# Packing the high and low rows of a 32-token tile into one stationary operand, and laying four weight pieces of the last chunk ahead

## The reference

```
D_MODEL = 2048; SEQ = 1024; DEC_SEQ = 32

y_prompt = y_prompt + rms_norm(jnp.einsum('btm,md->btd', mp, w_out[l]), norm_post[l])
y_sample = y_sample + rms_norm(jnp.einsum('btm,md->btd', ms, w_out[l]), norm_post[l])

def rms_norm(x, gain):
    xf = x.astype(jnp.float32)
    y = xf * lax.rsqrt(jnp.mean(xf * xf, axis=-1, keepdims=True) + NORM_EPS)
    return (y * gain.astype(jnp.float32)).astype(x.dtype)
```

## Time and profile before

| | before |
|---|---|
| median of 3 runs | 2122.13 us (2121.92 to 2123.47) |
| the profiled execution's own time | 2120.78 us |
| its span | 2119.0 us |
| PE busy | 2059.1 us, 97% |
| DVE busy | 1078.6 us, 51% |
| ACT busy | 684.1 us, 32% |
| mean granted TensorE clock | 0.992 |

### The profile page before, as it was taken

The page is one execution under the profiler, slowest core; times in us unless marked ns, Lnnn a source line. Parts: engine busy times, 40 slices in busy tenths (PEclk is TensorE's granted clock), DMA queues, the critical chain, the costliest instruction groups (busy, mean ns, idle before and its releaser), DMA issues.

```text
span 2119.0 us, 31442 instructions
## 1 busy us (share of the span) xinstructions
PE 2059.1 (97%) x13280; PEld 1864.0 (88%) x13280; DVE 1078.6 (51%) x2001; ACT 684.1 (32%) x1226; POOL 9.4 (0%) x28
## 2 busy tenths in 40 slices
PE   4999999999999999999999999999999999999996
PEld 4998989898898989999999999999999978887885
DVE  7457676776777676434233332544244562233224
ACT  6223333333434332323222231433133452222221
POOL 1000000000000000000000000000000000000000
PEclk8999999999999999999999999999999999999998
DMA  6256577675757577122221313121322442336323
GB/s 245 75 116 134 122 160 151 138 152 127 148 128 158 121 160 150 51 66 61 51 76 41 91 37 79 42 51 51 67 50 51 142 171 99 104 127 236 123 78 124
DMA packets 601476, 230.75 MB, mean 109 GB/s; under 512 B 395944, under 2 KB 575928, under 8 KB 599576
## 3 DMA queue, kind: packets, MB, share of 16 engines
q1 hardware_dynamic: 600168, 220.76, 41.6%
q0 software_dynamic: 1168, 7.99, 1.0%
HBM read 167.52 MB, written 64.37 MB: 109 GB/s over the span
## 4 chain that ended last, share of the span: by engine, by line
PE 83%; DVE 10%; ACT 3%; DMA 2%; issue 1%; SPq 0%; DVEq 0%; ACTq 0%
PE ps L853 18%; PE ps L854 17%; PE ps L855 17%; PE ps L1048 6%; PE ps L1047 6%; PE ps L1046 6%; DVE arena L1435 3%; PE ps L944 3%; PE ps L1030 3%; PE ps L963 3%; PE ps L911 2%; PE ps L1001 2%; DVE arena L1429 2%; ACT arena L1226 1%; DVE arena L1443 1%
## 5 line engine op out<-in xcount | busy, mean ns | idle before, releaser
L853 PE MATMUL ps<-act_hi,w_hi 128*128 128x352 f32 x2688 | 885.6, 329 | 9.6 <-DVE arena L1370 5.9
L854 PE MATMUL ps<-act_lo,w_hi 128*128 128x352 f32 x2688 | 870.0, 324 | 0.0
L855 PE MATMUL ps<-act_hi,w_lo 128*128 128x352 f32 x2688 | 869.8, 324 | 0.0
L853 PEld LDWEIGHTS ps<-act_hi,w_hi 128*128 128x128 f32 x2688 | 507.4, 189 | 41.1 <-issue 28.5
L855 PEld LDWEIGHTS ps<-act_hi,w_lo 128*128 128x128 f32 x2688 | 507.7, 189 | 0.0
L854 PEld LDWEIGHTS ps<-act_lo,w_hi 128*128 128x128 f32 x2688 | 507.7, 189 | 0.0
L1346 DVE TENSOR_TENSOR w_lo<-w_raw,w_hi 128x512 fp32r<-128x512 f32 x352 | 240.3, 684 | 335.8 <-ACT w_hi L1204 239.7
L1046 PE MATMUL ps<-w_hi,act_hi 128*128 128x512 f32 x576 | 227.2, 394 | 4.9 <-DVE w_lo L1346 2.9
L1048 PE MATMUL ps<-w_hi,act_lo 128*128 128x512 f32 x576 | 229.4, 398 | 0.0
L1047 PE MATMUL ps<-w_lo,act_hi 128*128 128x512 f32 x576 | 228.6, 397 | 0.0
L1132 ACT ACTIVATE w_hi<-w_raw 128x512 fp32r<-128x512 f32 x224 | 139.3, 624 | 214.0 <-DMA w_raw<-in_w_in_dram 213.9
(11 more groups left out here) (120 smaller groups left out, 1618.0 us busy)
## 6 DMA issues: line engine op xcount, KB each, us to landing
w_raw<-in_w_in_dram SPq DMA_DIRECT2D x176, 256.0 KB, 3.0
w_raw<-in_w_out_dram SPq DMA_DIRECT2D x128, 256.0 KB, 2.7
weight_scratch<-arena SPq DMA_DIRECT2D x216, 128.0 KB, 3.8
arena<-weight_scratch SPq DMA_DIRECT2D x54, 512.0 KB, 4.3
w_raw<-in_w_in_dram SPq DMA_DIRECT2D x96, 128.0 KB, 2.4
arena<-in_x_prompt_dram SPq DMA_DIRECT2D x8, 1024.0 KB, 7.0
out_dram<-arena SPq DMA_DIRECT2D x14, 512.0 KB, 2.9
value_scratch<-arena SPq DMA_DIRECT2D x48, 132.0 KB, 3.4
```

What stands on the lines that cost most here:

```text
L853: mm(bank(g, GN), wh, ah, start=(k == 0), stop=False)
L854: mm(bank(g, GN), wh, al, start=False, stop=False)
L855: last = mm(bank(g, GN), wl, ah, start=False, stop=(k == KT - 1))
```

## The change

- **Two matmuls a piece for the sample's tile.** When chunk 3 is done, tile 0's columns of act_hi are free. ACT copies the sample's high part to columns 0-31 of that place and its low part to columns 32-63 (pair, semaphore paired). For tile 8 one stationary operand, pair_rows, then holds both: a matmul against w_hi and one against w_lo give the high rows' product in PSUM partitions 0-31 and the low rows' in 32-63. The low x low product, which the kernel before leaves out, is now added too. Columns 64-127 are whatever tile 0 left, and their rows are not read.
- **A join.** At each of the four chunk ends ACT copies partitions 32-63 of the bank to the tile's rows of y (low_moved), DVE adds the bank's rows 0-31 (joined), ACT squares from y into the bank, and DVE applies the gain to y.
- **The last chunk's end.** LAST_PIECES is 8: PE goes through pieces 0 to 7 with all tiles, then tile by tile over eight pieces. The last four of these are laid ahead during chunk 6: SP loads them into act_lo's columns of tile 3 (as res_lo), ACT makes their high parts in act_hi's columns of tile 3, DVE their low parts in place (late_piece, late_high, late_low). A lone tile takes these four first and the pieces 8 to 11 of the ring after them (the list alone).
- **Small moves.** The gain's load (gain_chunk) is issued after piece 7 instead of piece 9, and the 96 columns of padding behind act_hi and act_lo, with their two memsets, are gone.

```
-LAST_PIECES = 4
+LATE = 4
+LAST_PIECES = LATE + RING
...
-        act_hi_t = place("act_hi", [P, ACT_N + P - DEC], F32R, ACT_N + P - DEC)
-        act_lo_t = place("act_lo", [P, ACT_N + P - DEC], F32R, ACT_N + P - DEC)
-        act_hi = act_hi_t[:, 0:ACT_N].rearrange("p (k t) -> p k t", k=KT)
-        act_lo = act_lo_t[:, 0:ACT_N].rearrange("p (k t) -> p k t", k=KT)
+        act_hi = place("act_hi", [P, KT, TOK], F32R, ACT_N)
+        act_lo = place("act_lo", [P, KT, TOK], F32R, ACT_N)
+        pair_rows = act_hi[:, :, 0:P]
...
+        def late_part(t, i):
+            return t[:, 4 * i:4 * i + 4, 3 * P:4 * P]
+        def piece_view(ap):
+            return ap.rearrange("p (k c) -> p k c", c=P)
...
+            def late_piece(i):
+                sp.wait_ge(y_done, TILES_BEFORE[NCH])
+                g, n = CHUNKS[-1]
+                sp.dma_start(late_part(res_lo, i),
+                             piece_view(w_out_v[:, KORD[KT - LATE + i], PIECE * n:PIECE * n + PIECE])).then_inc(late_in[i], 16)
...
-                for pos in range(RING, KT):
+                for pos in range(RING, KT if c + 1 < len(CHUNKS) else KT - LATE):
                     out_piece(c, pos)
-                    if pos == 9:
+                    if pos == 7:
                         gain_chunk(c)
                     if c == NCH and pos >= 8:
                         residual(pos - 8)
                     if c == NCH + 1 and pos in (7, 9, 11, 13):
                         late_residual(pos // 2 - 3)
+                    if c == NCH + 2 and pos < RING + LATE:
+                        late_piece(pos - RING)
                 if c + 1 < len(CHUNKS):
...
+            alone = list(range(KT - LATE, KT)) + list(range(KT - LAST_PIECES, KT - LATE))
...
-                t0 = TOK * k + P * TOKSETS[g][j]
-                th, tl = act_hi_t[:, t0:t0 + P], act_lo_t[:, t0:t0 + P]
-                mm(bank(s % 8), th, w_hi[:, slot, :], start=(pos == 0), stop=False)
-                mm(bank(s % 8), th, w_lo[:, slot, :], start=False, stop=False)
-                last = mm(bank(s % 8), tl, w_hi[:, slot, :], start=False, stop=(pos == KT - 1))
-                if pos == KT - 1:
+                tt = TOKSETS[g][j]
+                out, wh, wl = bank(s % 8), w_hi[:, slot, :], w_lo[:, slot, :]
+                if c + 1 == len(CHUNKS) and pos >= KT - LATE:
+                    i = pos - KT + LATE
+                    out, wh, wl = piece_view(out), late_part(act_hi, i), late_part(act_lo, i)
+                end = KT - 1 if c + 1 < len(CHUNKS) else alone[-1]
+                if tt == TT:
+                    if c == NCH and pos == 0:
+                        pe.wait_ge(paired, 2)
+                    mm(out, pair_rows[:, k, :], wh, start=(pos == 0), stop=False)
+                    last = mm(out, pair_rows[:, k, :], wl, start=False, stop=(pos == end))
+                else:
+                    th, tl = act_hi[:, k, P * tt:P * tt + P], act_lo[:, k, P * tt:P * tt + P]
+                    mm(out, th, wh, start=(pos == 0), stop=False)
+                    mm(out, th, wl, start=False, stop=False)
+                    last = mm(out, tl, wh, start=False, stop=(pos == end))
+                if pos == end:
                     last.then_inc(y_done, 1)
                 elif j == len(TOKSETS[g]) - 1:
...
-                    for pos in range(KT - by_tile, KT):
-                        if j == 0:
+                    for pos in alone if by_tile else ():
+                        if j == 0 and pos < KT - LATE:
                             pe.wait_ge(lo_made, P3 + KT * c + pos + 1)
+                        elif j == 0:
+                            pe.wait_ge(late_lo, pos - KT + LATE + 1)
                         out_mm(c, pos, j)
...
+                out, src = y[0:rows, j, PIECE * n:PIECE * n + PIECE], bank(s % 8, 512, rows)
                 act.wait_ge(y_done, s + 1)
-                fn(y[0:rows, j, PIECE * n:PIECE * n + PIECE], bank(s % 8, 512, rows), ACT.Square,
+                if tt == TT:
+                    fn(out, ps[DEC:2 * DEC, 512 * (s % 8):512 * (s % 8) + 512], ACT.Copy).then_inc(low_moved, 1)
+                    act.wait_ge(joined, n + 1)
+                    out, src = src, out
+                fn(out, src, ACT.Square,
                    accum_out=ssq_y[0:rows, 4 * tt + n:4 * tt + n + 1]).then_inc(y_sq, 1)
+            def late_high(i):
+                act.wait_ge(late_in[i], 16)
+                fn(late_part(act_hi, i), late_part(res_lo, i), ACT.Copy).then_inc(late_hi, 1)
+            def pair(src, at):
+                act.wait_ge(y_done, TILES_BEFORE[NCH])
+                fn(act_hi[:, :, at:at + DEC], src[:, :, SEQ:TOK].bitcast(F32), ACT.Copy).then_inc(paired, 1)
             def following_high(c, pos):
-                if pos + RING < KT:
+                if pos + RING < (KT if c + 1 < len(CHUNKS) else KT - LATE):
                     out_high(c, pos + RING)
...
+                    if c == NCH + 2 and KT - LATE - 2 <= pos < KT - 2:
+                        late_high(pos - KT + LATE + 2)
                 for j in range(0 if last_chunk else 1, tiles):
                     squares(c, j)
+                    if c == NCH - 1 and j == tiles - 1:
+                        pair(act_hi, 0)
+                        pair(act_lo, DEC)
...
+                o = y[0:rows, j, PIECE * n:PIECE * n + PIECE]
+                src = bank(s % 8, 512, rows)
+                if rows == DEC:
+                    dve.wait_ge(low_moved, n + 1)
+                    v.tensor_tensor(o, src, o, ALU.add).then_inc(joined, 1)
+                    src = o
                 dve.wait_ge(y_sq, s + 1)
-                v.tensor_tensor(y[0:rows, j, PIECE * n:PIECE * n + PIECE], bank(s % 8, 512, rows),
-                                post_gain[c % 2][0:rows, :], ALU.mult).then_inc(y_out, 1)
+                v.tensor_tensor(o, src, post_gain[c % 2][0:rows, :], ALU.mult).then_inc(y_out, 1)
...
+            def late_low(i):
+                dve.wait_ge(late_hi, i + 1)
+                v.tensor_tensor(late_part(act_lo, i), late_part(res_lo, i), late_part(act_hi, i).bitcast(F32),
+                                ALU.subtract).then_inc(late_lo, 1)
             def following_low(c, pos):
-                if KT * c + pos + RING < KT * len(CHUNKS):
+                if KT * c + pos + RING < KT * len(CHUNKS) - LATE:
```

More of the change, by code:

```diff
@@ L359, in build @@
         ACT_N = KT * TOK
-        act_hi_t = place("act_hi", [P, ACT_N + P - DEC], F32R, ACT_N + P - DEC)
-        act_lo_t = place("act_lo", [P, ACT_N + P - DEC], F32R, ACT_N + P - DEC)
-        act_hi = act_hi_t[:, 0:ACT_N].rearrange("p (k t) -> p k t", k=KT)
-        act_lo = act_lo_t[:, 0:ACT_N].rearrange("p (k t) -> p k t", k=KT)
+        act_hi = place("act_hi", [P, KT, TOK], F32R, ACT_N)
+        act_lo = place("act_lo", [P, KT, TOK], F32R, ACT_N)
+        pair_rows = act_hi[:, :, 0:P]
         res_hi = place("res_hi", [P, KT, TOK], F32, 0, 0)
-        res_lo = place("res_lo", [P, KT, TOK], F32, 0, ACT_N + P - DEC)
+        res_lo = place("res_lo", [P, KT, TOK], F32, 0, ACT_N)
         ring0 = at[0]
@@ L477, in build @@
         last_stored = sem("last_stored")
+        late_in = [sem(f"late_in{i}") for i in range(LATE)]
+        late_hi, late_lo = sem("late_hi"), sem("late_lo")
         mx_hi, mx_lo = sem("mx_hi"), sem("mx_lo")
+        paired, low_moved, joined = sem("paired"), sem("low_moved"), sem("joined")
         post_in = [sem("post_in0"), sem("post_in1")]
@@ L1301, in _ @@
             v = nc.vector
-            v.memset(act_hi_t[:, ACT_N:].bitcast(F32), 0.0)
-            v.memset(act_lo_t[:, ACT_N:].bitcast(F32), 0.0).then_inc(zeroed, 1)
             v.memset(qbd[:, :], 0.0).then_inc(zeroed, 1)
@@ L1373, in tile_out @@
                     if u == 0:
-                        dve.wait_ge(zeroed, 2)
+                        dve.wait_ge(zeroed, 1)
                     for h in range(2):
@@ L1591, in _ @@
                         mixed_lo(pos + 4)
+                    if c == NCH + 2 and KT - LATE - 2 <= pos < KT - 2:
+                        late_low(pos - KT + LATE + 2)
                     if c == NCH and 4 <= pos < 4 + 2 * len(TOKSETS[0]):
```

## The result

| | before | after |
|---|---|---|
| median of 4 runs each, same chip | 2122.03 us (2120.60 to 2123.47) | 2091.26 us (2089.07 to 2091.59) |
| ratio, with its 95% interval | | 0.985 (0.9836 to 0.9863) |
| span of the profiled execution | 2119.0 us | 2089.7 us |
| PE's first matmul of the output projection | 1693.20 us | 1682.08 us |
| PE's last matmul | 2103.21 us | 2075.85 us |

The fourth row says where to look: 11.1 us are gained before the output projection begins, in a part of the program that the change leaves as it was.

A forecast was written before the change was run, and what follows sets the result against it. PE, dense at 0.2326 us a matmul, was taken to bound the output projection, with DVE the bound after PE's final matmul. The terms summed to -19.1 us, so 2101.7 us for the profiled execution, 2103.0 us as median; range 2099.5 to 2107.5.

The forecast's parts named there:

- The rest: Loading the gain two pieces earlier and dropping the padding's memsets was claimed to cost 0.
- matmuls removed: Tile 8 in four chunks: 64 fewer at 0.2326 us each, the remaining matmul at the same price; -14.9 us.
- weight stall: Last chunk, PE's wait for the last ring piece: 3.1 us lost before, 0.3 us staying.
- low clock in chunk 7: The 1.2 GHz stretch behind the last chunk's 3.1 us stop goes away with that stop: -1.7 us.
- pair: Tile 8 of chunk 4: PE waits for ACT's two copies of the sample; +0.6 us, between 0 and 1.5.
- stores of chunk 4: Start of chunk 5: PE arrives sooner and waits longer behind ACT's wait for stores; +1.7 us (0.9 to 2.6).
- tail: After PE's last matmul: no DVE queue with eight lone pieces, end 9.9 us after tile 8 is done; -2.0 us.
- if a low clock follows a stop there: Sign that the prediction is wrong: 1.2 GHz behind PE's stop for the stores at chunk 5's start.
- Pieces laid ahead: Four weight pieces loaded and split during chunk 6: cost 0, hidden; without cover 1.3 us a piece.
- rival of the four-run operand: Reading laid-ahead pieces breaks the stream for 56 matmuls; 2116 us at twice the price; chance 0.04, slower than before 0.02.
- chunk 4 is bound by the DMA engines: Rival: stores end hardly sooner, 3.1 to 3.6 us lost, perhaps a low clock; 2105.5 us, chance 0.20.

The follow-up runs named there:

- e1: Kernel after with 96 unused columns put back behind act_hi and behind act_lo, so tensors lie at the old addresses: 2104.19 us (ratio 0.9915).
- e2: Kernel before without its 96 padding columns and two memsets, tile 8's last block reading 32 columns: 2108.68 us (ratio 0.9936).
- e9: Kernel after with no piece laid ahead (LATE = 0), the two matmuls a piece kept: 2096.43 us (ratio 0.9879).
- e8: Kernel after with three matmuls a piece for the sample's tile again, no pair copies and no join: 2099.50 us (ratio 0.9896).
- e10: Kernel after with chunk 4's residual loads and finishing of tiles 0 to 3, and with them the stores, two pieces earlier: 2085.38 us (ratio 0.9828).
- e12: Kernel after with 128 bytes of unused space between w_lo and w_hi: 2093.21 us (ratio 0.9864).
- e4: Kernel after with 96 unused columns behind act_lo only, so the weight ring lies 384 bytes higher: 2085.50 us.
- e7: Kernel after with 32 unused columns ahead of act_hi, so every address moves by 128 bytes and distances stay: 2088.07 us.

## Why the prediction was wrong

**The step that failed** is "The rest. The gain's load two pieces earlier and the missing memsets: 0". I took the missing padding for its memsets and never asked what it moves. It moves act_lo against act_hi, and so changes the pace of 8064 matmuls that I hadn't looked at: 12.9 us (after against e1), 13.1 us (e2 against before). Bound up with it is that I held the 0.2326 us of the earlier trace rows for a constant of the shape; it is a value of this shape at these addresses. No rival of mine had such a mechanism, so the range was too narrow on its low side by 8 us.

**The terms themselves** are tried at the old addresses, in e1 against the kernel before. e1 came to 2104.19 us, where the forecast was 2103.0, and its span fell by 17.0 us where the sum said 19.1. Each figure is from one profiled execution of each.

| term | forecast | measured, e1 against before |
|---|---|---|
| 64 matmuls | -14.9 | -14.9 at 232.5 ns |
| weight stall and low clock in chunk 7 | -4.5 | 4.74 us lost before, 0.13 now: -4.6 |
| pair | +0.6 | +0.96 |
| stores of chunk 4 | +1.7 | 0.61 us lost before, 3.13 now: +2.5 |
| tail | -2.0 | last matmul to end 15.8, then 13.8: -2.0 |
| the start | 0 | output projection begins at 1694.23 us, not 1693.20: +1.0 |

("Lost" is a chunk's length less its matmuls at the distance of its dense part.) The terms come to the 17.0 us.

- *Matmuls removed, what stays costs the same:* right. A fuller stationary operand costs nothing that shows.
- *The weight stall:* right to 0.1 us; 0.20 us of idle time stay at 2054.79 us, for the forecast's 0.3. e9 shows the other side.
- *The low clock behind it:* right in e1, but the reason that I gave doesn't carry it. I tied it to the stop of 3.1 us. e9 stopped for 2.71 us at the same place and kept 1.00; the kernel after stopped for 0.38, 1.49 and 0.22 us at the start of chunk 5 and got 0.50. e1 stopped there for 2.35 and 0.23 us and kept 1.00. By my own sign, "if a low clock follows a stop there", the kernel after speaks against me.
- *Pieces laid ahead:* cost 0 forecast, and right. In the kernel after, from 2061.18 to 2063.98 us twelve such matmuls take 233.3 ns each, and the twelve of the ring behind them, to 2066.76 us, 231.7: 1.6 ns for each of 56, 0.1 us in all. The rival of the four-run operand falls.
- *The pair:* 0.62 us of idle time in the kernel after and 0.58 in e1, there 0.96 us with what a restart costs. It is the copies' wait, since e8, without them, has none.
- *The stores:* 2.5 us lies at the high end of the range (0.9 to 2.6), but only half of the mechanism is the forecast one. PE does come to chunk 5 sooner, since chunk 4 takes 2.8 us less in e1. The stores, which I had end 0.5 to 2.2 us sooner, end 56.1 us after the start of chunk 4 in e1, and before it was 56.2. That is what the rival "chunk 4 is bound by the DMA engines" said, and e1's loss is its price of 3.1 us. In the kernel after they end at 55.2, which is 1930.0 on the clock of before and inside my 1928.8 to 1930.5; the low clock that this rival named stands behind that stop. And e2 and e8, where no matmul is removed, lose more in chunk 5 than the kernel before does, because their stores end later still. So that this term came out near its size is in part luck, of which execution of which kernel was profiled. That the wait is the stores' is shown by e10, which takes it away. The Trainium skill ("Trainium Kernel Development and Optimization", Key Constraints) says that the queues' transfers interleave on the same 16 engines; the share of 0.87 and e10's weight piece of 9.13 us agree with it.
- *The tail:* DVE went through the forecast order at the forecast times. ACT's copy of tile 8 starts at 2076.29 us and DVE ends at 2086.19 (its last row starts at 2083.72 and takes 2.47), which is the forecast 9.9 us, with DVE idle between lone tiles.

**Where 12.9 us went** that 16.6 could have been: the output projection began 12.15 us earlier than in e1 (1694.23 to 1682.08), and chunks 1 to 3 gave 0.9 us more; a low clock in chunk 0 took 1.5 back, and the chunks 4 to 7 gave 0.7. In the input projection PE waited 3.3 us longer, mostly for DVE, and so it is in every kernel: 9.6 to 10.1 us of idle time in the four with a rest of 128, 12.7 to 13.1 in those with a rest of 0, and 12.1 in e12. That DVE paces some of the layer's stages is read from those idle times and was not tried.

## What to carry to other kernels

A change that removes or adds a buffer also moves every buffer behind it. Before costing such an edit at nothing, compare the addresses of operands between which PE alternates. In the result, compare the distance of starts in stretches that the edit doesn't touch; one run with unused space in the old place separates the two effects. Here that is worth 13 us, nearly as much as the 64 matmuls, and the kernel before could have had it without the change.

When a stage gets shorter, don't let the transfers that it waits for get shorter with it unless a row says so: here PE came 2.8 us sooner and the stores hardly (e1). And where loads, stores and weights share a crowded stretch, moving one of them can hand the wait to another, as in e10.

## What the runs showed of the hardware

- **The pace of fp32r matmuls depends on where two operands lie to each other.** Activations whose high and low parts are 128 bytes off a multiple of 256: 161.5 ns a matmul of 352 columns as the moving operand, 232.7 ns one of 512 columns with them as the stationary one. At a multiple of 256: 159.4 and 231.1. In e1 the pattern of before came back. Each row of act_hi is 4224 bytes, 16.5 times 256, so neighbouring blocks k always differ by 128; how this and the distance act together is open, and so is the mechanism. The Trainium skill ("TensorE: Matmul & The Clock Gate", section "Back-to-back issue gap") has a formula in the column count alone, for what it calls the isolated gap: 352 / 2.4 + 2.5 = 149 ns, and 216 ns for 512 columns. For a stream with weight loads it gives 131 ns at 512 columns. Every mean here lies above these, and by that rule e1 and the kernel after would take the same time, where 12.9 us lie between them.
- **The weights' distance does less**: 0.5 ns for 128 bytes in the input projection (e12).
- **The low clock comes and goes.** A stretch of 3.4 us at 0.50 stands in some executions behind stops of 1.5 to 3.4 us and is missing behind stops of like length in others (after and e2 against e1 and e9). It costs 1 to 2 us. No row read here tells them apart beforehand.
- **The start** of the output projection differs by some 2 us between kernels with the same pace (1679.96 in e2, 1680.03 in e4, 1682.08 after). The first hundred matmuls already end at 42.6 us in the kernel before and at 44.2 after; the extremes are 42.5 (e10) and 45.1 (e7). Why wasn't tried.
